# Stick-breaking attention heads taken two at a time in a two-block transformer kernel

## The chip, the cores and the metric

The kernel runs on one core of a Trainium2 chip. The metric is the device time of one execution in microseconds (us). A core has five engines, each with its own list of instructions: TensorE (PE, matmuls), VectorE (DVE), ScalarE (ACT), GpSimd (POOL) and SyncE (SP, which here only issues transfers). They meet through semaphores: an instruction can wait until a semaphore has reached a value, and can raise one when it is done. A list is worked off strictly in order, so an instruction that waits holds up everything behind it on its engine.

## The reference

Two transformer blocks run over 512 tokens of width 1024 (the second one in two layers). The change lies in the first layer of the second block, in its stick-breaking attention of 8 heads of width 64:

```python
def _stick_breaking(q, k, v):
    for blk in range(seq // QBLOCK):               # QBLOCK = 128
        t0, t1 = blk * QBLOCK, (blk + 1) * QBLOCK
        z = einsum('bhtd,bhsd->bhts', q[:, :, t0:t1], k[:, :, :t1]) * scale
        mask = arange(t1)[None, :] < arange(t0, t1)[:, None]
        log1m = where(mask, -softplus(z), 0.0)
        suffix = cumsum(log1m, axis=3, reverse=True)
        a = where(mask, exp(z + suffix), 0.0)
        outs.append(einsum('bhts,bhsd->bhtd', a, v[:, :, :t1]))
```

q and k are root-mean-square normalised per head before it. Beside this attention the same layer computes `y_a = u * mixed`, where `mixed` is a masked product of 128x128 matrices, and then multiplies both halves by an output matrix. Everything is float32.

## The kernel before

All weights stream in as chunks of 128 x 1024. SyncE loads a chunk into one of 4 buffers (`RAW`). ScalarE's `hi()` copies it, rounded, to one of 3 buffers (`WH`, L800), and VectorE's `lo()` writes what the rounding left (`WL`, L1260). A gemm then makes 3 matmuls for each of 8 slices (high x high, high x low, low x high, L279 to L281), 24 in all, on one chunk. `hi()` of chunk n waits until the gemm of chunk n - 3 is done, because it writes that chunk's buffer. Chunks have a fixed order, so each call of `hi()` and of `lo()` means the next chunk.

The 8 heads are worked in rounds `n` = 0 to 9, written out by hand in `tensor`, `scalar` and `vector`, each in a function `even()`. Work on a head goes through these steps:

- `st_a`: TensorE multiplies keys and queries (L602), 1280 score columns for a head (transposed and triangular in blocks of 128): four diagonal blocks in bank 2, the rest in banks 3 and 7. A head's key and query are 64 rows high, in rows 0 to 63 for even heads and 64 to 127 for odd ones.
- `st_z`: VectorE adds the mask to the diagonal blocks (L1560) and copies the rest (L1565) into the head's row of scores, `ZR`. ScalarE's `st_soft` computes the softplus in absolute value (L1041, L1045), exp (L1047) and log (L1049) in `SPR`; VectorE's L1568 combines. A change between exp and log, root or gelu costs ScalarE a table load.
- GpSimd adds blocks of the softplus into `TS`; TensorE's `st_b` forms the sums from the right (L615, and L622 with a matrix of ones), in banks 2, 3 and 7 again.
- `st_zd`: VectorE subtracts them from the scores (L1575); `st_exp`: ScalarE's exp (L1034).
- `st_c`: TensorE multiplies the values (L633), 64 columns wide, into the lower or upper half of bank 6. After an odd head ScalarE (`close`) and VectorE move the bank out.

Between the steps stand the gemms of the next queries and keys (`even_job`, chunks `eq` and `ek`), later of `u` (`eu`). For each pair of heads, `head_norm` (TensorE's 2-column sums L562, VectorE's L1539, ScalarE's root L809, VectorE's reciprocal) and `head_apply` (TensorE spreads the factor, L575; VectorE multiplies, L1548) normalise query and key. `st_a` waits for them through the semaphore `qkn`. A bank is reused when `open_bank` has seen the semaphore of its last reader. Before round 0, `spatial()` fills banks 4, 5, 0 and 1, which VectorE empties with four additions (L1626).

The attention of the first block (`scores`, `values`, lines L382 and L463) works on two heads at a time, in alternating halves of the array.

Of the kernel before, what the change touches and what calls it, by code (L numbers as in the profile page):

```python
# [9 lines left out]
S = 512  # L10
# [3 lines left out]
ALU = mybir.AluOpType  # L14
# [125 lines left out]
def build(nc, W, X, CV, PAR, CON, OH, LNG, LNB, SGB, SGW, RB, OUT):  # L140
    scr = nc.dram_tensor("bias_scratch", (16, 640), F32)

    with ExitStack() as ctx:
# [76 lines left out]
        QE, KE, VE, MX, VG = ar.take(4, S), ar.take(4, S), ar.take(4, S), ar.take(4, S), ar.take(4, S)  # L220
        LG, LB = CSB[:, 0:512], CSB[:, 512:1024]
        SQ2 = CSB[:, 0:512]
        SW, SBT, st, HN = ar.take(8, 128), ar.take(4, 128), ar.take(4, 16), ar.take(64)
        Z01, SP0, TS = ar.take(2, 1280), ar.take(1280), ar.take(384)
        ZR = [Z01[:, 0, :], Z01[:, 1, :], ARENA[:, 8192:8192 + 1280]]
        SPR = [SP0, ARENA[:, 8192 + 1280:8192 + 2560]]
# [44 lines left out]
        free = {}  # L271

        def tensor(e):
# [320 lines left out]
            def st_a(h):  # L594
                c, r0 = h // 2, 64 * (h % 2)
                e.wait_ge(sem["qkn"], 2 * c + 2)
                parts = [[(i, 128 * i, 128 * i + 128, 128 * i) for i in range(4)],
                         [(0, 128, 512, 0), (2, 384, 512, 384)], [(1, 256, 512, 0)]]
                for p, (part, b) in enumerate(zip(parts, (2, 3, 7))):
                    open_bank(b)  # L600
                    for i, q0, q1, c0 in part:
                        t = e.matmul(ps(b, c0, c0 + q1 - q0), KE[r0:r0 + 64, c, 128 * i:128 * i + 128],  # L602
                                     QE[r0:r0 + 64, c, q0:q1], start=True, stop=True)
                    t.then_inc(sem["sqk"])
                    free[b] = (("z", 3 * h + p + 1),)

            def st_b(h):
                L = SPR[h % 2]
# [4 lines left out]
                for p, ((lo, hi), b) in enumerate(zip(PIECES, (2, 3, 7))):  # L613
# [6 lines left out]
                for part, b in zip(later, (2, 3, 7)):  # L620
                    for m, (c0, c1, src) in enumerate(part):
                        t = e.matmul(ps(b, c0, c1), ON, src, start=False, stop=(m == len(part) - 1))  # L622
                    if part:
                        t.then_inc(sem["suf"])

            def st_c(h):
                r0 = 64 * (h % 2)
                jobs = [(i, 128 * i, 128 * i + 128, 128 * i) for i in range(4)]
                jobs += [(i, 128 * (i + 1), 512, LATE[i][0]) for i in (0, 1, 2)]
                e.wait_ge(sem["za"], h + 1)  # L630
                open_bank(6)
                for m, (i, q0, q1, z0) in enumerate(jobs):
                    t = e.matmul(PSB[6][r0:r0 + 64, q0:q1], VE[:, i, 64 * h:64 * h + 64], ZR[h % 3][:, z0:z0 + q1 - q0],  # L633
                                 start=(m == 0), stop=(m == 6))
                t.then_inc(sem["spv"])
                if h % 2:
                    free[6] = (("o_lo", 8 + h // 2 + 1),)
# [4 lines left out]
            def even():  # L642
# [12 lines left out]
                for n in range(10):  # L655
                    if 1 <= n <= 8:
                        st_b(n - 1)
                    if n < 8:
                        st_a(n)
                    if n == 0:  # L660
                        gemm([even_job(2, 0)], B)
                        gemm([even_job(3, 1)], B)
                    elif n in (1, 3, 5):
                        c = (n + 1) // 2
                        head_norm(c)
                        if c < 3:
                            gemm([even_job(2 * c + 2, 0)], B)
                        else:
                            gemm([(("eu", 0), 0, ("u_rr", 1))], B)
                        head_apply(c)  # L670
                    elif n in (2, 4):
                        gemm([even_job(n + 3, 1)], B)
                    elif n < 9:
                        gemm([(("eu", n - 5), (n - 5) % 2, ("u_rr", n - 4))], B)
                    if n >= 2:
                        if n == 2:
                            e.wait_ge(sem["tok"], 12)
                        st_c(n - 2)
# [111 lines left out]
        def scalar(e):  # L790
# [241 lines left out]
            def st_exp(h):  # L1032
                e.wait_ge(sem["zd"], 3 * h + 3)
                e.activation(ZR[h % 3], ZR[h % 3], ACT.Exp).then_inc(sem["za"])  # L1034

            def st_soft(h):
                L, Z = SPR[h % 2], ZR[h % 3]
                e.wait_ge(sem["z"], 3 * h + 1)
                if h > 1:
                    e.wait_ge(sem["suf"], 3 * (h - 2) + 3)  # L1040
                e.activation(L[:, 0:512], Z[:, 0:512], ACT.Abs).then_inc(sem["abs"])  # L1041
                for p, b in ((1, 3), (2, 7)):
                    lo, hi_ = PIECES[p]
                    e.wait_ge(sem["sqk"], 3 * h + p + 1)
                    e.activation(L[:, lo:hi_], ps(b, 0, hi_ - lo), ACT.Abs).then_inc(sem["abs"])  # L1045
                e.wait_ge(sem["abs"], 3 * h + 3)
# [11 lines left out]
            def even():  # L1058
# [30 lines left out]
                for n in range(10):  # L1089
                    if 1 <= n <= 8:  # L1090
                        st_exp(n - 1)
                    if n == 7:
                        e.wait_ge(sem["spg"], 4)
                    if n < 8:
                        st_soft(n)
                    if n == 0:
                        even_sq(2)
                        hi()
                        even_sq(3)
                    elif n in (1, 3, 5):  # L1100
                        c = (n + 1) // 2
                        head_sqrt(c)
                        hi()
                        if c < 3:
                            even_sq(2 * c + 2)
                        else:
                            eu(0)
                    elif n in (2, 4):
                        hi()
                        even_sq(n + 3)  # L1110
                    elif n < 9:
                        hi()
                        eu(n - 5)
                    if n >= 3 and n % 2:
                        m = (n - 3) // 2
                        close(A[0][:, 4 + m, :], ("spv", n - 1))
# [135 lines left out]
        def vector(e):  # L1252
# [302 lines left out]
            def st_z(h):  # L1555
                Z = ZR[h % 3]
                e.wait_ge(sem["sqk"], 3 * h + 1)
                if h > 2:
                    e.wait_ge(sem["spv"], h - 2)
                e.tensor_tensor(blocks(Z[:, 0:512], 4), blocks(ps(2), 4), bcast(cc("smask"), 4),  # L1560
                                ALU.add).then_inc(sem["z"])
                for p, b in ((1, 3), (2, 7)):
                    c0, c1 = PIECES[p]
                    e.wait_ge(sem["abs"], 3 * h + p + 1)
                    e.tensor_copy(Z[:, c0:c1], ps(b, 0, c1 - c0)).then_inc(sem["z"])  # L1565
                e.wait_ge(sem["z"], 3 * h + 3)
                e.wait_ge(sem["sln"], h + 1)
                e.scalar_tensor_tensor(SPR[h % 2], Z, 0.0, SPR[h % 2], ALU.max, ALU.add).then_inc(sem["sp"])  # L1568

            def st_zd(h):  # L1570
                Z = ZR[h % 3]
                for p, b in enumerate((2, 3, 7)):
# [12 lines left out]
            def even():  # L1585
# [42 lines left out]
                for n in range(10):  # L1628
                    if 1 <= n <= 8:
                        st_zd(n - 1)  # L1630
                    if n < 8:
                        st_z(n)
                    if n == 0:
                        even_rr(2, 0)
                        lo()
                        even_rr(3, 1)
                    elif n in (1, 3, 5):
                        c = (n + 1) // 2
                        head_norm(c)
                        lo()  # L1640
# [5 lines left out]
                    elif n in (2, 4):  # L1646
                        lo()
                        even_rr(n + 3, 1)
                    elif n < 9:
                        lo()  # L1650
                        eu(n - 5)
# [178 lines left out]
        def gpsimd(e):  # L1830
# [44 lines left out]
            for h in range(8):  # L1875
                L = SPR[h % 2]
                e.wait_ge(sem["sp"], h + 1)
                if h:
                    e.wait_ge(sem["suf"], 3 * h)
# [4 lines left out]
            e.wait_ge(sem["spv"], 8)  # L1884
# [131 lines left out]
```

## Time and profile before

| | us |
|---|---|
| median of 3 runs | 1923.31 (1922.28 to 1924.86) |
| profiled execution | 1924.35 |
| its span | 1922.5 |
| TensorE busy | 1871.0 (97%) |
| VectorE busy | 955.1 (50%) |
| ScalarE busy | 753.5 (39%) |
| GpSimd busy | 76.6 (4%) |
| mean granted TensorE clock | 0.991 |

The profile comes from one execution. "Busy" is the time in which an engine works on at least one instruction; what matters for the time is the chain of work that ended last and the waits on it. The granted clock is the share of full TensorE speed (2.4 GHz) that the chip allowed; 0.5 is 1.2 GHz. Float32 matmuls of the attention appear as two records each, so seven matmuls show as x14. The rounds changed here lie between 799 and 941 us.

### The profile page before, as it was taken

To read this page: it belongs to the slowest core of one execution; us is meant where nothing else is said; L and a number is where in the kernel's file an instruction comes from. 1 tells how busy PE (TensorE), PEld (TensorE's weight loads), DVE (VectorE), ACT (ScalarE), POOL (GpSimd) and SP (SyncE) were. 2 spreads that over 40 slices of the span, in tenths; PEclk is the share of its full clock that TensorE was granted. 3 is DMA by queue.
4 is the path that set the end of the run, shared out by engine and by line. 5 is a ranking of instruction groups with operands and counts; after the bars stand their busy time and mean duration, and the time that the engine had idled before them with its cause. 6 is when DMAs were issued, how large, how long until landed. Compare 5 with 4: busy or idle time off the path is not lost.

```text
span 1922.5 us, 21105 instructions
## 1 busy us (share of the span) xinstructions
PE 1871.0 (97%) x8624; PEld 1512.8 (79%) x8624; DVE 955.1 (50%) x1363; ACT 753.5 (39%) x1080; POOL 76.6 (4%) x94
## 2 busy tenths in 40 slices
PE   3999999899999999999999999999999999999999
PEld 2788788778888888777788888888876788888887
DVE  7377636553434455645554444345734554344343
ACT  4366542342323243466543323233446443232231
POOL 5100000000000000000000000000001000000000
PEclk9999999899999999999999999999999999999999
DMA  7455553222222223110123222222321132222322
GB/s 256 163 173 184 167 173 132 88 77 99 99 97 101 88 99 115 66 45 23 56 98 102 96 99 99 99 88 99 98 77 44 55 102 96 99 99 91 105 90 77
DMA packets 55120, 197.65 MB, mean 103 GB/s; under 512 B 6400, under 2 KB 6656, under 8 KB 55024
## 3 DMA queue, kind: packets, MB, share of 16 engines
q1 hardware_dynamic: 52272, 188.24, 28.7%
q0 software_dynamic: 2320, 7.31, 1.4%
q8 instruction: 69, 1.13, 0.2%
q10 hardware_dynamic: 432, 0.74, 0.1%
q14 instruction: 27, 0.22, 0.0%
HBM read 194.13 MB, written 2.14 MB: 102 GB/s over the span
## 4 chain that ended last, share of the span: by engine, by line
PE 93%; DVE 4%; ACT 2%; DMA 0%; issue 0%; POOL 0%; SPq 0%; ACTq 0%; DVEq 0%
PE ps L279 26%; PE ps L281 26%; PE ps L280 26%; PE ps L315 2%; PE ps L316 2%; PE ps L317 2%; DVE RAW L1268 1%; PE ps L382 1%; PE ps L615 1%; PE ps L703 1%; DVE WL L1260 1%; PE ps L602 1%; PE ps L633 1%; PE ps L333 1%; PE ps L622 1%; ACT WH L800 0%
## 5 line engine op out<-in xcount | busy, mean ns | idle before, releaser
L279 PE MATMUL ps<-R0h,WH 128*128 128x512 f32 x1200 | 472.0, 393 | 20.4 <-POOL R0l L1837 17.9
L1260 DVE TENSOR_TENSOR WL<-RAW,WH 128x1024 fp32r<-128x1024 f32 x303 | 372.4, 1233 | 215.9 <-ACT WH L800 212.2
L800 ACT ACTIVATE WH<-RAW 128x1024 fp32r<-128x1024 f32 x303 | 317.6, 1052 | 392.8 <-PE ps L281 339.5
L280 PE MATMUL ps<-R0l,WH 128*128 128x512 f32 x1200 | 468.5, 390 | 0.0
L281 PE MATMUL ps<-R0h,WL 128*128 128x512 f32 x1200 | 468.3, 390 | 0.0
L279 PE MATMUL ps<-R1h,WH 128*128 128x512 f32 x1064 | 420.5, 395 | 7.9 <-POOL R1l L1867 2.8
L280 PE MATMUL ps<-R1l,WH 128*128 128x512 f32 x1064 | 417.0, 392 | 0.0
L281 PE MATMUL ps<-R1h,WL 128*128 128x512 f32 x1064 | 416.8, 392 | 0.0
L279 PEld LDWEIGHTS ps<-R0h,WH 128*128 128x128 f32 x1200 | 226.0, 188 | 74.5 <-issue 15.2
L281 PEld LDWEIGHTS ps<-R0h,WL 128*128 128x128 f32 x1200 | 226.1, 188 | 47.5
L280 PEld LDWEIGHTS ps<-R0l,WH 128*128 128x128 f32 x1200 | 226.2, 188 | 46.1
L279 PEld LDWEIGHTS ps<-R1h,WH 128*128 128x128 f32 x1064 | 201.5, 189 | 58.2 <-issue 11.8
L281 PEld LDWEIGHTS ps<-R1h,WL 128*128 128x128 f32 x1064 | 201.5, 189 | 42.6
L280 PEld LDWEIGHTS ps<-R1l,WH 128*128 128x128 f32 x1064 | 201.7, 190 | 41.2
L1307 DVE TENSOR_TENSOR XT<-ps,XT 128x512 f32<-128x512 f32 x80 | 55.3, 691 | 192.0 <-PE ps L281 192.0
L1299 DVE TENSOR_TENSOR R0l<-TMP,R0h 128x512 fp32r<-128x512 f32 x117 | 81.0, 692 | 125.3 <-ACT R0h L997 87.4
L995 ACT ACTIVATE TMP<-TMP 128x512 f32<-128x512 f32 x64 | 40.5, 633 | 201.5 <-DVE TMP L1481 201.5
L1481 DVE SCALAR_TENSOR_TENSOR TMP<-ps,SQ 128x512 f32<-128x512 f32 x64 | 44.2, 690 | 78.0 <-PE ps L281 78.0
L1310 DVE SCALAR_TENSOR_TENSOR XT<-ps,mod,XT 128x512 f32<-128x512 f32 x40 | 29.9, 750 | 87.7 <-PE ps L281 87.7
L1268 DVE CUSTOM_DVE_ANT_0 RAW<-RAW,CSB,par 128x1024 f32<-128x1024 f32 x48 | 67.0, 1408 | 0.0
L1469 DVE TENSOR_TENSOR TMP<-TMP 128x512 f32<-128x512 f32 x32 | 22.1, 692 | 64.1 <-ACT TMP L982 64.1
L315 PE MATMUL ps<-WH,R1h 128*128 128x512 f32 x128 | 51.1, 399 | 0.0
(270 smaller groups left out, 1413.6 us busy)
## 6 DMA issues: line engine op xcount, KB each, us to landing
RAW<-in_W SPq DMA_DIRECT2D x351, 512.0 KB, 3.2
XT<-in_X SPq DMA_DIRECT2D x4, 512.0 KB, 7.8
ARENA<-bias_scratch POOLq DMA_DIRECT2D x8, 256.0 KB, 4.4
XT<-in_X POOLq DMA_DIRECT2D x8, 256.0 KB, 3.7
out_x<-XT SPq DMA_DIRECT2D x8, 256.0 KB, 2.0
ARENA<-bias_scratch POOLq DMA_DIRECT2D x8, 128.0 KB, 3.6
con<-in_CON POOLq DMA_DIRECT2D x1, 578.0 KB, 6.0
CSB<-in_CV ACTq DMA_DIRECT2D x1, 512.0 KB, 5.9
```

The source lines that it names most:

```text
L279: e.matmul(ps(b), wh, hi, start=first, stop=False)
L280: e.matmul(ps(b), wh, lo, start=False, stop=False)
L281: return e.matmul(ps(b), wl, hi, start=False, stop=last)
L315: e.matmul(ps(b), h1, wh, start=(k == 0), stop=False)
L316: e.matmul(ps(b), h1, wl, start=False, stop=False)
L800: e.activation(WH[:, n % NHL, :], RAW[:, i % NRAW, :], ACT.Copy).then_inc(sem["w_hi"])
L995: e.activation(TMP[:, j, :], TMP[:, j, :], ACT.Square).then_inc(sem["mlp_sq"])
L1260: e.tensor_tensor(WL[:, s, :], RAW[:, i % NRAW, :], r32(WH[:, s, :]), ALU.subtract).then_inc(sem["w_lo"])
L1268: e.tensor_tensor_reduce(RAW[:, r, :], RAW[:, r, :], CSB[:], 1.0, par[:, c0:c0 + 1], ALU.mult, ALU.add, mod_col(j)).then_inc(sem["ada"])
L1299: e.tensor_tensor(dst[1][:, k, :], src, r32(dst[0][:, k, :]), ALU.subtract).then_inc(sem[done])
L1307: e.tensor_tensor(XT[:, k, :], ps(b), XT[:, k, :], ALU.add).then_inc(sem[done])
L1481: e.scalar_tensor_tensor(TMP[:, j, :], ps(b), 0.0, SQ[:], ALU.max, ALU.mult).then_inc(sem["mlp_rr"])
```

## The change

Scores and values are computed for two heads at once. `st_a(m)` writes the scores of heads 2m and 2m + 1: the even head into banks 2, 3 and the left half of 7, the odd head into 4, 5 and the right half of 7, with matmuls of lower and upper rows mostly in turn, and a wait before the second write to bank 7. `st_c(c)` writes the values of both heads in turn. The sums of even heads (`st_b`) go to banks 4, 5, 6, those of odd ones to 2, 3, 7. There are now four rows of scores (`ZR`) and two sets of block sums (`TSR`). In the arena `VG`, `SW` and `SBT` share their place with one row of softplus and two rows of scores. ScalarE takes absolute values from the scores that VectorE wrote, in one instruction. The order of the steps within the rounds changes on three engines.

```diff
+        SP1, ZR2, ZR3 = (ARENA[:, at0 + 1280 * n:at0 + 1280 * n + 1280] for n in range(3))
+        Z01, SP0, TSR = ar.take(2, 1280), ar.take(1280), ar.take(2, 384)
+        ZR = [Z01[:, 0, :], Z01[:, 1, :], ZR2, ZR3]
...
-            def st_a(h):
+            def st_a(m):
+                def part(e_, i, q0, q1, b, c0):
+                    r = slice(64 * e_, 64 * e_ + 64)
+                    return e.matmul(ps(b, c0, c0 + q1 - q0), KE[r, m, 128 * i:128 * i + 128], QE[r, m, q0:q1],
+                                    start=True, stop=True)
+                def diag(e_, i):
+                    return part(e_, i, 128 * i, 128 * i + 128, 2 + 2 * e_, 128 * i)
+                e.wait_ge(sem["qkn"], 2 * m + 2)
+                for b in (7, 4):
                     open_bank(b)
+                part(0, 1, 256, 512, 7, 0).then_inc(sem["sqk"])
+                diag(1, 0)
+                diag(1, 1)
+                for b in (3, 5):
+                    open_bank(b)
+                part(0, 0, 128, 512, 3, 0)
+                part(1, 0, 128, 512, 5, 0)
+                part(0, 2, 384, 512, 3, 384).then_inc(sem["sqk"])
+                part(1, 2, 384, 512, 5, 384).then_inc(sem["sqk"])
+                open_bank(2)
+                diag(0, 0)
+                e.wait_ge(sem["sqk"], 6 * m + 1)
+                part(1, 1, 256, 512, 7, 256).then_inc(sem["sqk"])
+                diag(0, 1)
+                for i in (2, 3):
+                    t0 = diag(0, i)
+                    t1 = diag(1, i)
...
             def st_b(h):
+                banks = (2, 3, 7) if h % 2 else (4, 5, 6)
...
-            def st_c(h):
+            def st_c(c):
-                e.wait_ge(sem["za"], h + 1)
+                e.wait_ge(sem["za"], 2 * c + 2)
                 open_bank(6)
                 for m, (i, q0, q1, z0) in enumerate(jobs):
+                    for h in (2 * c, 2 * c + 1):
+                        r0 = 64 * (h % 2)
+                        t = e.matmul(PSB[6][r0:r0 + 64, q0:q1], VE[:, i, 64 * h:64 * h + 64],
+                                     ZR[h % 4][:, z0:z0 + q1 - q0], start=(m == 0), stop=(m == 6))
...
                 for n in range(10):                      # TensorE
-                    if 1 <= n <= 8:
-                        st_b(n - 1)
-                    if n < 8:
-                        st_a(n)
+                    if n % 2:
+                        if n < 9:
+                            st_b(n - 1)
+                    elif n < 8:
+                        st_a(n // 2)
+                    else:
+                        st_b(7)
...
-                    if n >= 2:
+                    if n in (2, 4, 6):
+                        st_b(n - 1)
+                    if n % 2 and n >= 3:
...
-                        st_c(n - 2)
+                        st_c((n - 3) // 2)
...
                 for n in range(10):                      # ScalarE
-                    if 1 <= n <= 8:
-                        st_exp(n - 1)
-                    if n < 8:
-                        st_soft(n)
+                    if n == 8:
+                        hi()
+                        st_exp(7)
+                    elif n % 2 == 0:
+                        hi()
+                        st_soft(n)
+                    elif n < 9:
+                        if n > 1:
+                            st_exp(n - 2)
+                        if n < 6:
+                            head_sqrt((n + 1) // 2)
+                        hi()
+                        st_exp(n - 1)
+                        st_soft(n)
...
                 for n in range(10):                      # VectorE
-                    if 1 <= n <= 8:
+                    if n == 8:
+                        st_zd(7)
+                    elif n % 2 == 0:
+                        st_z(n)
+                        st_z(n + 1)
+                    elif n < 9:
+                        if n > 1:
+                            st_zd(n - 2)
                         st_zd(n - 1)
+                        if n < 6:
+                            head_norm((n + 1) // 2)
+                    if n < 9:
+                        lo()
                     if n < 8:
-                        st_z(n)
+                        st_sp(n)
```

`st_sp` is the combination of the softplus, before the last lines of `st_z`. After it VectorE goes on with `even_rr` or `eu` and `head_apply` as before.

How the order moves on ScalarE at round 0, before:

```order
L800 ACTIVATE WH<-RAW 128x1024 [waits mm,raw2]
L1041 ACTIVATE ARENA<-ARENA 128x512 [waits z]
L1045 ACTIVATE ARENA<-ps3 128x512 [waits sqk]
L1045 ACTIVATE ARENA<-ps7 128x256 [waits sqk]
L1047 ACT_TABLE_LOAD
L1047 ACTIVATE ARENA<-ARENA 128x1280 [waits abs]
L1049 ACT_TABLE_LOAD
L1049 ACTIVATE ARENA<-ARENA 128x1280 [waits sxp]
```

And after, at the same place (L832 is the weight copy, L1073 the absolute value, L1075 the exp, L1077 the log, L1062 the squares for the head sums, L841 the root):

```order
L832 ACTIVATE WH<-RAW 128x1024 [waits mm,raw2]
L832 ACTIVATE WH<-RAW 128x1024 [waits mm,raw3]
L1073 ACTIVATE ARENA<-ARENA 128x1280 [waits z]
L1075 ACT_TABLE_LOAD
L1075 ACTIVATE ARENA<-ARENA 128x1280 [waits abs]
L1077 ACT_TABLE_LOAD
L1077 ACTIVATE ARENA<-ARENA 128x1280 [waits sxp]
L1062 ACTIVATE TMP<-ARENA 128x512 [waits hss,eqk] x2
```

The weight copy from `raw3` stood behind the softplus, between the two squares; now it stands ahead of the softplus. It waits (`mm`) for the first gemm of round 0.

VectorE from the sums of head 0 to the next pair's halves, before (L1575 subtracts the sums, L1568 combines the softplus of head 1, L1539 and L1543 are `head_norm`, L1533 is `even_rr`, L1548 `head_apply`):

```order
L1575 TENSOR_TENSOR ARENA<-ARENA,ps7 128x256 [waits suf]
L1560 TENSOR_TENSOR ARENA<-ps2,con 128x512 [waits sqk]
L1565 COPY ARENA<-ps3 128x512 [waits abs]
L1565 COPY ARENA<-ps7 128x256 [waits abs]
L1568 SCALAR_TENSOR_TENSOR ARENA<-ARENA 128x1280 [waits sln,z]
L1539 TENSOR_SCALAR ARENA<-ps2 128x8 [waits hss] x2
L1543 RECIPROCAL ARENA<-ARENA 128x16 [waits hsqrt]
L1260 TENSOR_TENSOR WL<-RAW,WH 128x1024 [waits w_hi]
L1533 TENSOR_TENSOR ARENA<-ps0,SQ 128x512 [waits mm]
L1548 SCALAR_TENSOR_TENSOR ARENA<-ARENA,par,ps3 128x512 [waits hspr]
L1548 SCALAR_TENSOR_TENSOR ARENA<-ARENA,par,ps7 128x512 [waits hspr]
```

And after, in the same order of steps (L1600, L1564, L1568, L1285, L1593, L1558, L1573):

```order
L1600 TENSOR_TENSOR ARENA<-ARENA,ps6 128x256 [waits suf]
L1564 TENSOR_SCALAR ARENA<-ps2 128x8 [waits hss] x2
L1568 RECIPROCAL ARENA<-ARENA 128x16 [waits hsqrt]
L1285 TENSOR_TENSOR WL<-RAW,WH 128x1024 [waits w_hi]
L1593 SCALAR_TENSOR_TENSOR ARENA<-ARENA 128x1280 [waits z,sln]
L1558 TENSOR_TENSOR ARENA<-ps0,SQ 128x512 [waits mm]
L1573 SCALAR_TENSOR_TENSOR ARENA<-ARENA,par,ps3 128x512 [waits hspr]
L1573 SCALAR_TENSOR_TENSOR ARENA<-ARENA,par,ps7 128x512 [waits hspr]
L1585 TENSOR_TENSOR ARENA<-ps2,con 128x512 [waits sqk]
```

The combination stood ahead of the two `head_norm` instructions; now it stands between them and `head_apply`.

TensorE's first scores, before (five rows for head 0):

```order
L602 MATMUL ps2<-ARENA 128x128 [waits hn,qkn]
L602 MATMUL ps2<-ARENA 128x128 x3
L602 MATMUL ps3<-ARENA 128x384 [waits qkn]
L602 MATMUL ps3<-ARENA 128x128
L602 MATMUL ps7<-ARENA 128x256 [waits qkn]
```

And after, for heads 0 and 1:

```order
L602 MATMUL ps7<-ARENA 128x256 [waits mx,qkn]
L602 MATMUL ps4<-ARENA 128x128 x2
L602 MATMUL ps3<-ARENA 128x384 [waits mx,qkn]
L602 MATMUL ps5<-ARENA 128x384
L602 MATMUL ps3<-ARENA 128x128
L602 MATMUL ps5<-ARENA 128x128
L602 MATMUL ps2<-ARENA 128x128 [waits hn]
L602 MATMUL ps7<-ARENA 128x256 [waits sqk]
```

The first scores now wait for `mx`, which VectorE's additions of L1626 raise (L1651 after).

## Rows read from the trace of the kernel before

**Rows 1.** The page: busy time by engine, and the chain that ended last by engine.

```profile
PE 1871.0 (97%) x8624; PEld 1512.8 (79%) x8624; DVE 955.1 (50%) x1363; ACT 753.5 (39%) x1080; POOL 76.6 (4%) x94
PE 93%; DVE 4%; ACT 2%; DMA 0%; issue 0%; POOL 0%; SPq 0%; ACTq 0%; DVEq 0%
```

**Rows 2.** The view by windows, the changed rounds: length, busy by engine, clock, DMA.

```profile
core 0: us, PE busy (x) PEld busy (x) DVE busy (x) ACT busy (x) POOL busy (x), PEclk, DMA share, GB/s
799.00:946.00 147.00, 144.41 (x760) 109.96 (x757) 75.28 (x112) 93.14 (x103) 14.10 (x26) 0.95 0.11 38
```

**Rows 3.** TensorE's waits from 799 to 946 us: total, times, longest.

```profile
PE ps L279 <- DVE ARENA L1626: 2.1, 1, 2.1
PE ps L615 <- DVE ARENA L1548: 0.5, 1, 0.5
```

**Rows 4.** TensorE's timeline, round 1 and part of 2: start, us, engine, line.

```profile
821.13 2.46 PE L602 MATMUL ps<-ARENA 64*128 64x128 f32 x14
823.52 1.95 PE L562 MATMUL ps<-con,TMP 128*128 128x2 f32 x16
825.33 0.48 PE L279 MATMUL ps<-R1h,WH 128*128 128x512 f32 x1
...
830.99 1.97 PE L575 MATMUL ps<-con,ARENA 128*64 128x128 f32 x32
...
844.73 2.38 PE L633 MATMUL ps<-ARENA 128*64 128x128 f32 x14
```

**Rows 5.** TensorE's timeline, first block: values, then scores, two heads each.

```profile
194.95 2.37 PE L463 MATMUL ps<-ARENA 128*64 128x512 f32 x16
197.25 2.95 PE L382 MATMUL ps<-ARENA 64*128 64x512 f32 x16
```

**Rows 6.** VectorE's timeline, rounds 0 and 1.

```profile
801.63 2.48 DVE L1626 TENSOR_TENSOR ARENA<-ps,ARENA 128x512 f32<-128x512 f32 x4
...
811.40 1.49 DVE L1568 SCALAR_TENSOR_TENSOR ARENA<-ARENA 128x1280 f32<-128x1280 f32 x1 [4.50 <-ACT ARENA L1049]
812.81 0.68 DVE L1533 TENSOR_TENSOR ARENA<-ps,SQ 128x512 f32<-128x512 f32 x1
...
829.85 0.23 DVE L1539 TENSOR_SCALAR ARENA<-ps 128x8 f32<-128x8 f32 x2
...
833.06 1.40 DVE L1548 SCALAR_TENSOR_TENSOR ARENA<-ARENA,par,ps 128x512 f32<-128x512 f32 x2
```

**Rows 7.** ScalarE's timeline: softplus, weight copy, root, and a gelu of `eu`.

```profile
806.14 1.28 ACT L1047 ACT_TABLE_LOAD   x1
807.44 1.27 ACT L1047 ACTIVATE ARENA<-ARENA 128x1280 f32<-128x1280 f32 x1
808.73 1.28 ACT L1049 ACT_TABLE_LOAD   x1
810.02 1.27 ACT L1049 ACTIVATE ARENA<-ARENA 128x1280 f32<-128x1280 f32 x1
...
814.07 1.04 ACT L800 ACTIVATE WH<-RAW 128x1024 fp32r<-128x1024 f32 x1
...
823.05 0.63 ACT L1041 ACTIVATE ARENA<-ARENA 128x512 f32<-128x512 f32 x1
823.59 0.85 ACT L1045 ACTIVATE ARENA<-ps 128x512 f32<-128x512 f32 x2
...
830.12 0.22 ACT L809 ACTIVATE ARENA<-ARENA 128x16 f32<-128x16 f32 x1 [0.49 <-DVE ARENA L1539]
...
897.58 0.63 ACT L1054 ACTIVATE TMP<-TMP 128x512 f32<-128x512 f32 x1 [0.59 <-DVE TMP L1580]
```

**Rows 8.** TensorE around its two slow stretches, then windows with the granted clock.

```profile
803.65 0.77 PE L279 MATMUL ps<-R1h,WH 128*128 128x512 f32 x1 [2.13 <-DVE ARENA L1626]
...
850.71 2.46 PE L602 MATMUL ps<-ARENA 64*128 64x128 f32 x14
853.10 2.60 PE L562 MATMUL ps<-con,TMP 128*128 128x2 f32 x16
...
804.00:810.00 6.00, 6.00 (x15) 4.69 (x15) 1.72 (x4) 5.22 (x6) 0.00 (x0) 0.51 0.01 3
853.00:861.00 8.00, 8.00 (x30) 6.75 (x30) 3.03 (x7) 7.29 (x9) 1.29 (x3) 0.57 0.00 1
```

More of the change, by code:

```diff
@@ L592, in spatial @@
                     free[b] = (("mx", gp + 1),)
-            def st_a(h):
[L595 to L599, printed above, removed]
-                    open_bank(b)
[L601 to L605, printed above, removed]
+            def st_a(m):
[7 more added lines that the diff above has]
+                for b in (7, 4):
+                    open_bank(b)
+                part(0, 1, 256, 512, 7, 0).then_inc(sem["sqk"])
[15 more added lines that the diff above has]
+                    t1 = diag(1, i)
+                t0.then_inc(sem["sqk"])
+                t1.then_inc(sem["sqk"])
+                for b, z in ((2, 1), (3, 2), (7, 6), (4, 4), (5, 5)):
+                    free[b] = (("z", 6 * m + z),)
@@ L612, in st_b @@
                 e.wait_ge(sem["sp"], h + 1)
-                for p, ((lo, hi), b) in enumerate(zip(PIECES, (2, 3, 7))):
+                for p, ((lo, hi), b) in enumerate(zip(PIECES, banks)):
                     open_bank(b)
@@ L619, in st_b @@
                 e.wait_ge(sem["ts"], 3 * h + 3)
-                for part, b in zip(later, (2, 3, 7)):
+                for part, b in zip(later, banks):
                     for m, (c0, c1, src) in enumerate(part):
@@ L1097, in even @@
                         even_sq(2)
-                        hi()
                         even_sq(3)
[L1100 to L1109, printed above, removed]
+                    elif n < 5:
                         even_sq(n + 3)
                     elif n < 9:
-                        hi()
                         eu(n - 5)
@@ L1555, in st_z, with st_sp @@
             def st_z(h):
[L1556 to L1560, printed above, removed]
+                Z, up = ZR[h % 4], h % 2
+                if h > 3:
+                    e.wait_ge(sem["spv"], h // 2 - 1)
+                e.wait_ge(sem["sqk"], 6 * (h // 2) + 5 + up)
+                e.tensor_tensor(blocks(Z[:, 0:512], 4), blocks(ps(2 + 2 * up), 4), bcast(cc("smask"), 4),
                                 ALU.add).then_inc(sem["z"])
[L1562 to L1565, printed above, removed]
+                e.tensor_copy(Z[:, 512:1024], ps(3 + 2 * up)).then_inc(sem["z"])
+                e.tensor_copy(Z[:, 1024:1280], ps(7, 256 * up, 256 * up + 256)).then_inc(sem["z"])
+            def st_sp(h):
+                e.wait_ge(sem["sln"], h + 1)
                 e.wait_ge(sem["z"], 3 * h + 3)
-                e.wait_ge(sem["sln"], h + 1)
-                e.scalar_tensor_tensor(SPR[h % 2], Z, 0.0, SPR[h % 2], ALU.max, ALU.add).then_inc(sem["sp"])
+                e.scalar_tensor_tensor(SPR[h % 2], ZR[h % 4], 0.0, SPR[h % 2], ALU.max, ALU.add).then_inc(sem["sp"])
             def st_zd(h):
-                Z = ZR[h % 3]
-                for p, b in enumerate((2, 3, 7)):
+                Z = ZR[h % 4]
+                for p, b in enumerate((2, 3, 7) if h % 2 else (4, 5, 6)):
                     c0, c1 = PIECES[p]
@@ L1875, in gpsimd @@
             for h in range(8):
-                L = SPR[h % 2]
+                L, TS = SPR[h % 2], TSR[:, h % 2, :]
                 e.wait_ge(sem["sp"], h + 1)
-                if h:
-                    e.wait_ge(sem["suf"], 3 * h)
+                if h > 1:
+                    e.wait_ge(sem["suf"], 3 * h - 3)
                 e.tensor_tensor(TS[:, 256:384], L[:, 896:1024], L[:, 384:512], ALU.add).then_inc(sem["ts"])
```

46 lines of the change are left out of this document (16 added, 30 removed).

## The prediction

> **What bounds the kernel now.** I read the page first: TensorE is busy 97% of the span and holds 93% of the chain that ended last [rows 1]. A microsecond off or on TensorE in any stage is therefore a microsecond of the time, unless something else already holds the engine there. The change touches one stage, the stick-breaking heads, so I read next the windows from 799 to 946 us: TensorE 144.4 of 147 us, ScalarE 93, VectorE 75 [rows 2]. The waits of that stretch say what else there is: TensorE waited for data only twice, 2.1 us for an addition on VectorE and 0.5 us for the scaled heads [rows 3]. So the other two engines have slack on average; whether they still have it in the new order is the whole question. Third comes TensorE's timeline of one round, for prices [rows 4]. Last the granted clock: two stretches of this stage run at half speed (1.2 instead of 2.4 GHz), one after the 2.13 us wait, one after a score group of 64 rows followed by the sixteen 2-column matmuls of the head sums [rows 8].
>
> **Part 1: paired scores and values.** Before, a head's scores use 64 rows of the array and take 2.46 us; a head's values use 64 columns and take 2.38 us [rows 4]. There are 8 of each: 19.7 and 19.0 us. The first block already works in pairs: its values of two heads, alternating between the output halves, as many columns in all as two of these groups, took 2.37 us together, and its scores of two heads 2.95 us [rows 5]. One group of one head costs what two of them do when they alternate. The new scores alternate a little better than those of the first block but are cut into 14 matmuls instead of 8, with one wait of TensorE for its own first matmul, so I take 2.6 us a pair, and 2.5 us for a pair of values (bounds for each 2.37 and 2.95). Saved: 19.7 - 4 x 2.6 = 9.3 and 19.0 - 4 x 2.5 = 9.0, together 18.3 us (bounds 15.1 and 19.8). If pairs did not overlap here it would be nothing.
>
> **Part 2: the start.** TensorE reaches the first scores at 799.06 (803.65 - 2.13 - 2.46, [rows 8, 4]). Before, it does them first and then waits 2.13 us for bank 0. Now they also write bank 4, which is free only once the first addition of L1626 is done, 801.63 + 0.62 = 802.25 [rows 6]. The wait is 3.2 us: +1.1.
>
> **Part 3: round 0 to 1.** ScalarE's list now has the weight copy `hi()` ahead of the softplus of head 0, where before it was behind it. That copy waits until the first of the two gemms that follow is done (three weight buffers). Before, the softplus ran beside that gemm. Now, from its end: copy 1.04, absolute value 1.3 (before in pieces of 0.63 and 0.85), table load 1.28, exp 1.27, table load 1.28, log 1.27 [rows 7], VectorE's combination 1.49 [rows 6], 0.2 for the hops: 9.1 us. TensorE has one gemm of 5.5 us beside it (825.33 to 830.99 less its start, [rows 4]) and then stands at the sums of head 0: 3.6 us.
>
> **Part 4: odd rounds into even ones.** `st_a(1)` needs both normalised halves of the next pair, written by `head_apply`. Before, VectorE did the combination of its head, then `head_norm`, weight rest, `even_rr`, `head_apply`: no softplus lay between the head sums and the apply. Now the combination stands between `head_norm` and `head_apply`, and it waits for a softplus that ScalarE starts only after root, weight copy and the exp of the head before. From the end of the head sums: VectorE 0.23, root 0.22, copy 1.04, load 1.28, exp 1.27, absolute value 1.3, exp 1.27, load 1.28, log 1.27, combination 1.49, scaling 0.68, apply 1.40 [rows 6, 7], hops 0.3: 13.0. Beside it TensorE has gemm 5.5 and spread 1.9 [rows 4]: it waits 5.5 us before the second pair's scores. Before the third pair a value pair (2.5) lies in between as well: 3.0 us. Before the fourth pair the apply stands behind `eu(0)`, four more steps of 0.6 to 0.7 (one is in [rows 7]): 3.0 + 2.6 = 5.6 us.
> Round 7 to 8: from the end of the sums of head 6, VectorE's subtraction waits behind `eu(1)`, then exp, copy, exp, softplus (5.1) and combination follow; 11.4 us against gemm and value pair, 7.9: 3.5 us. In rounds 3, 5 and 7 the second head of a pair finishes about 0.5 us late: 1.5 in all.
>
> **Sum at full clock.** Waits added: 1.1 + 3.6 + 5.5 + 3.0 + 5.6 + 3.5 + 1.5 = 23.8 us; removed the 0.5 us of [rows 3], since scores now ask for the normalised halves at another place. 23.8 - 0.5 - 18.3 = +5.0 us. The extra tiles (a fourth row of scores, a second set of partial sums) take waits away on VectorE and GpSimd that were on nobody's path: 0. The whole-tile absolute value replaces three, from SBUF: within 0.2 us, counted above. TensorE's matmul count and every DMA stay.
>
> **The clock.** From 804 to 810 us the granted clock averages 0.51, from 853 to 861 it averages 0.57 [rows 8]; the first is all inside a slow stretch, the second holds 0.43 x 2 x 8 = 6.9 us of one. At half speed such a stretch costs half its length, 3.4 us, if TensorE is busy throughout. The trace shows a fall after a wait of 2.13 us and none after 0.5 us [rows 3, 8]. The new order has six waits of 3 us and more where there was one of 2.1. I count one fall for each, and take 2.6 us rather than 3.4, since part of a slow stretch lies in the wait itself or beside a ScalarE chain that then ends earlier relative to TensorE: 15.6 us. The two falls of before (6.8 us) lie in its own time; the second one stood behind half-row scores next to the head sums, a neighbourhood that is gone. Net +8.8 us; bounds 0 (as many falls as before) and 13.6 (six at 3.4).
> The Trainium skill (TensorE: Matmul & The Clock Gate, "Why this matters for your kernels") says to leave no idle gaps between matmul bursts, or the clock goes back to half. By that rule the savings of pairing are not there to be had while these gaps open; the trace agrees, by the fall after 2.13 us. The sum above does not rest on it.
>
> **Result.** 5.0 + 8.8 = +13.8 us on the profiled execution, 1924.35 us (span 1922.5 and 1.85 around it): 1938.2. The three timed runs have their median 1.0 lower, at 1923.31, so the forecast is 1937.
>
> A page and the trace differ on one price in the chains. The Trainium skill (ScalarE: Activation LUTs, "What ACT_TABLE_LOAD costs") puts a switch of table sets at about 2.66 us, 1.28 for the load and the rest for a drain. Here the load takes 1.28 us and the exp begins at its end (806.14 + 1.28, [rows 7]), so the measurement decides. By the page's figure each of the five chains, with two loads, would be 2.8 us longer, 14 us in all.
>
> **The rivals.**
> (a) *Falls of the clock stay at two or fewer.* Waits as above, clock as before: 1924.35 + 5.0 = 1929. For it: waits of 3 us are spread among full-array gemms, and paired matmuls fill the array. Against: the fall after 2.13 us. 15%.
> (b) *Faster: the chains are covered.* The mechanism is ScalarE's list in round 0 and VectorE's in round 1: if the weight copy did not wait for the gemm and the apply's chain took under 7.4 us, what TensorE has beside it, the waits would shrink to the start's +1.1 and the savings stand: 1924.35 - 18.3 + 1.1 = 1907. For it: ScalarE is busy 63% and VectorE 51% of the stage [rows 2]. Against: the chain is 13.0 us by single rows, and would have to lose 5.6. A partial form, chains some 3 us shorter in five places, would end near no change. Faster 4%, near no change 4%.
> (c) *The pairs do not overlap*, so the change does not do what it says on TensorE: 18.3 us are not saved, and the chains are no shorter: 1955. Against: [rows 5]. 3%.
> (d) *The table switches cost what the page says.* Two on each chain, 2.8 us longer in five places: 1951. Against: exp starts as the load ends in [rows 7]. 2%.
> The forecast itself, five or six falls, has 72%.
>
> **How the numbers follow.** The measurement of this kernel can tell about 0.2%, 3.8 us, from no change. Slower: forecast 72, (a) 15, (c) 3, (d) 2: 92%. Same 4%, faster 4%, both from (b). The likeliest case by its own bounds (savings 15.1 to 19.8 us, clock +5 to +13.6) runs from 1924.35 + 23.3 - 19.8 + 5 = 1933 to 1924.35 + 23.3 - 15.1 + 13.6 = 1946. The range takes in (a): 1928 to 1946.
>
> **What would show it.** In the profile after: the score group of a pair at 2.4 to 2.9 us with twice the matmuls, the value group at 2.4 to 2.6. TensorE's waits in the stage near 24 us instead of 2.6 of [rows 3], on VectorE's combination (round 1, round 8) and on its apply (rounds 2, 4, 6). Softplus of head 0 beginning about 1 us after the end of the first gemm. More stretches at half clock between 800 and 960. VectorE and ScalarE busy as before. Wrong would be: no wait over 1 us at the second pair's scores (b); a pair at 4.5 us or more (c); waits as said but the clock down only twice (a).

## The result, and the profile after

| | before | after |
|---|---|---|
| median of 7 runs, us | 1923.31 (1922.28 to 1924.86) | 1930.33 (1929.22 to 1934.18) |
| profiled execution, us | 1924.35 | 1930.21 |
| its span | 1922.5 | 1928.3 |

The ratio is 1.0041, 95% interval 1.0029 to 1.0052: slower by 0.4%. TensorE is busy less than before and waits more. From the profile page of the kernel after, to be set beside [rows 1]:

```profile
PE 1852.9 (96%) x8624; PEld 1502.4 (78%) x8624; DVE 953.4 (49%) x1363; ACT 754.6 (39%) x1066; POOL 72.9 (4%) x94
PE 89%; DVE 5%; ACT 4%; issue 1%; DMA 1%; POOL 0%; SPq 0%; ACTq 0%; DVEq 0%
```

TensorE is busy 18 us less in the whole and holds 89% of the chain that ended last instead of 93%. The waits of TensorE in the changed rounds, 795 to 955 us (total, times, longest; compare [rows 3]):

```profile
PE ps L602 <- DVE ARENA L1573: 14.0, 3, 5.8
PE ps L642 <- DVE ARENA L1593: 8.0, 4, 3.6
PE ps L602 <- DVE ARENA L1651: 3.3, 1, 3.3
```

That makes 25.3 us instead of 2.6: three waits of the scores (L602) for `head_apply` (L1573), four of the sums (L642) for the combination of the softplus (L1593), one for the first addition. TensorE's timeline shows where each stands, and what the paired groups take:

```profile
801.79 4.10 PE L602 MATMUL ps<-ARENA 64*128 64x256 f32 x28 [3.32 <-DVE ARENA L1651]
820.62 2.42 PE L642 MATMUL ps<-ARENA,con 128*128 128x512 f32 x6 [3.63 <-DVE ARENA L1593]
838.70 4.41 PE L602 MATMUL ps<-ARENA 64*128 64x256 f32 x28 [5.18 <-DVE ARENA L1573]
852.80 2.42 PE L642 MATMUL ps<-ARENA,con 128*128 128x512 f32 x6 [0.55 <-DVE ARENA L1593]
865.56 2.34 PE L661 MATMUL ps<-ARENA 128*64 128x128 f32 x28
870.88 4.64 PE L602 MATMUL ps<-ARENA 64*128 64x256 f32 x28 [2.99 <-DVE ARENA L1573]
906.11 4.64 PE L602 MATMUL ps<-ARENA 64*128 64x256 f32 x28 [5.79 <-DVE ARENA L1573]
920.51 2.42 PE L642 MATMUL ps<-ARENA,con 128*128 128x512 f32 x6 [0.48 <-DVE ARENA L1593]
935.40 3.84 PE L642 MATMUL ps<-ARENA,con 128*128 128x512 f32 x6 [3.35 <-DVE ARENA L1593]
948.29 0.50 PE L283 MATMUL ps<-R0h,WH 128*128 128x512 f32 x1
```

A value pair takes 2.34 to 2.39 us, as one head did in [rows 4]. A score pair takes 4.10 to 4.64 us: right behind its wait it runs at half clock. Windows, with the granted clock behind the POOL column; the last one holds the 3.63 us wait and the sums behind it, and there the clock stayed full:

```profile
802.00:805.00 3.00, 3.00 (x19) 2.46 (x21) 1.44 (x3) 0.00 (x0) 0.00 (x0) 0.50 0.03 5
835.00:843.00 8.00, 4.30 (x28) 3.71 (x28) 3.41 (x4) 1.73 (x3) 1.28 (x3) 0.57 0.00 0
870.00:877.00 7.00, 6.12 (x32) 5.10 (x33) 2.79 (x6) 1.56 (x3) 0.22 (x1) 0.51 0.02 4
904.00:911.00 7.00, 4.89 (x29) 4.15 (x30) 2.79 (x5) 1.40 (x2) 0.00 (x0) 0.51 0.00 0
816.60:827.00 10.40, 6.77 (x39) 5.14 (x38) 4.89 (x9) 5.59 (x7) 1.28 (x3) 1.00 0.01 4
```

ScalarE's timeline of round 0 shows the weight copy (L832) that now stands ahead, with the wait that held up the softplus behind it, and then the steps of the softplus end to end:

```profile
811.65 1.06 ACT L832 ACTIVATE WH<-RAW 128x1024 fp32r<-128x1024 f32 x1 [15.15 <-PE ps L285]
812.61 1.26 ACT L1073 ACTIVATE ARENA<-ARENA 128x1280 f32<-128x1280 f32 x1
813.89 1.28 ACT L1075 ACT_TABLE_LOAD   x1
815.19 1.28 ACT L1075 ACTIVATE ARENA<-ARENA 128x1280 f32<-128x1280 f32 x1
816.48 1.28 ACT L1077 ACT_TABLE_LOAD   x1
817.77 1.27 ACT L1077 ACTIVATE ARENA<-ARENA 128x1280 f32<-128x1280 f32 x1
```

The rounds, from the end of `spatial()` to the first output gemm, take 801.79 - 3.32 = 798.47 to 948.29, 149.8 us; before, from 799.06 to the row below, 142.2. They cost 7.6 us more. The rest of the span is 1.8 us shorter, in stretches that the change does not touch.

```profile
941.30 0.50 PE L279 MATMUL ps<-R0h,WH 128*128 128x512 f32 x1
```

### The profile page after: what moved, and what is told of

It is laid out like the page before. It is cut to its first block, busy times and chain, and to the rows that moved or that the text cites. A ratio compares the mean times of both kernels' runs of the same rounds, so it can differ in the third digit from the quotient of the medians.

```text
span 1928.3 us, 21089 instructions
## 1 busy us (share of the span) xinstructions
PE 1852.9 (96%) x8624; PEld 1502.4 (78%) x8624; DVE 953.4 (49%) x1363; ACT 754.6 (39%) x1066; POOL 72.9 (4%) x94
## 4 chain that ended last, share of the span: by engine, by line
PE 89%; DVE 5%; ACT 4%; issue 1%; DMA 1%; POOL 0%; SPq 0%; ACTq 0%; DVEq 0%
PE ps L283 26%; PE ps L284 25%; PE ps L285 25%; PE ps L319 2%; PE ps L320 2%; PE ps L321 2%; DVE RAW L1293 1%; PE ps L386 1%; PE ps L602 1%; PE ps L735 1%; PE ps L642 1%; ACT WH L832 1%; DVE WL L1285 1%; DVE ARENA L1593 1%; PE ps L337 1%
## 5 line engine op out<-in xcount | busy, mean ns | idle before, releaser
L1285 DVE TENSOR_TENSOR WL<-RAW,WH 128x1024 fp32r<-128x1024 f32 x303 | 372.2, 1232 | 215.4 <-ACT WH L832 211.5
L832 ACT ACTIVATE WH<-RAW 128x1024 fp32r<-128x1024 f32 x303 | 317.7, 1052 | 408.6 <-PE ps L285 354.7
```

The source lines that it names most:

```text
L832: e.activation(WH[:, n % NHL, :], RAW[:, i % NRAW, :], ACT.Copy).then_inc(sem["w_hi"])
L1285: e.tensor_tensor(WL[:, s, :], RAW[:, i % NRAW, :], r32(WH[:, s, :]), ALU.subtract).then_inc(sem["w_lo"])
```

## The experiments

The theory: pairing saves what it should on TensorE (T1), the time is lost in waits that come from the order of the steps on VectorE and ScalarE (T2), and in half-clock stretches that these waits bring (T3). The rivals: pairs do not save; the waits only move when one is removed; the half clock is independent of them. Each ratio below is to the kernel before, timed beside the run on the same chip: 1924.4 us beside the apply-first, copy-later, additions-first and fill runs, 1923.8 beside fill-all and exp-later, 1924.1 beside the others. The changed kernel's 1930.3 us stand beside 1923.3 (ratio 1.0041). So a difference to the changed kernel is uncertain by about 1 us more than the spread of the medians; where that matters the ratios decide.

### Is it the order? (T2)

**Apply first.** VectorE's `head_apply` ahead of the combination in rounds 1, 3 and 5, and in round 5 ahead of `eu(0)` as well:

```diff
-                    if n < 8:
+                    if n < 8 and n not in (1, 3, 5):
                         st_sp(n)
...
                             even_rr(2 * c + 2, 0)
-                        else:
+                        head_apply(c)
+                        st_sp(n)
+                        if c == 3:
                             eu(0)
-                        head_apply(c)
```

> The changed kernel, with VectorE's head_apply ahead of the softplus combination st_sp in rounds 1, 3 and 5. Theory (the lost time is waits made by the new order): the waits before the second, third and fourth pair's scores (5.2, 3.0, 5.8 us) shrink to about 1, 0 and 0 us, some 2 us come back before the sums in round 7, and the slow stretches behind them go, so the scores of pairs 1 to 3 take 2.6 us instead of 4.4 to 4.6: 1930.3 - 12 - 6 = 1912 us, 1908 to 1918. Rival (TensorE's own work grew: pairs do not save what they should, and waits only move elsewhere): within 3 us of 1930.

Measured 1913.87 us (ratio to before 0.995, 0.9937 to 0.9962), 16.5 less than the changed kernel. In its timeline the waits before the scores are 0.90, 0 and 0 us, and the scores of the later pairs run at full clock:

```profile
835.42 2.46 PE L602 MATMUL ps<-ARENA 64*128 64x256 f32 x28 [0.90 <-DVE ARENA L1573]
862.55 2.46 PE L602 MATMUL ps<-ARENA 64*128 64x256 f32 x28
889.78 2.46 PE L602 MATMUL ps<-ARENA 64*128 64x256 f32 x28
904.41 3.87 PE L642 MATMUL ps<-ARENA,con 128*128 128x512 f32 x6 [3.02 <-DVE ARENA L1593]
```

The last row is what came back: 3.0 us ahead of the sums in round 7, where 2 were expected, with a slow stretch behind them. One place in VectorE's list thus decides between slower and faster than before. TensorE's own work is not the cause.

**Copy later.** ScalarE in round 0 (VectorE's `lo()` likewise moves behind the combination and the step after it):

```diff
+                    elif n == 0:
+                        st_soft(n)
+                        hi()
```

> The changed kernel, with the softplus of head 0 ahead of the weight copy in round 0 on ScalarE, and its combination ahead of the rest of that chunk on VectorE. Theory: the 3.6 us wait before the sums of head 0 goes to under 1 us, no clock fall was tied to it: 1930.3 - 3.0 = 1927.3 us, 1925.5 to 1928.5. Rival (the later chain through the ScalarE copies takes it back at the next wait): 1930.

Measured 1927.88 us (ratio 1.002, 1.0011 to 1.0029; the changed kernel had 1.0029 to 1.0052). The 3.63 us wait before the sums of head 0 is gone; the later waits stay at 5.15, 3.02 and 5.79 us:

```profile
817.64 2.31 PE L642 MATMUL ps<-ARENA,con 128*128 128x512 f32 x6
835.60 4.64 PE L602 MATMUL ps<-ARENA 64*128 64x256 f32 x28 [5.15 <-DVE ARENA L1576]
```

What was won there was kept: 2.4 us by the medians, 3.5 against the kernel before beside each.

**Additions first.** VectorE ahead of round 0: the loop over L1651 before the last five `scale_x`.

> The changed kernel, with VectorE's four additions that empty banks 4, 5, 0, 1 ahead of its last five scalings. Theory: the 3.3 us wait before the first scores goes, and the slow stretch with it (1.7 us): 1930.3 - 5 = 1925.3 us, 1924 to 1927.5. Rival (the scalings, now later, delay the first pair's masks and the time returns in the wait before the sums of head 0, since ScalarE only starts after the first gemm anyway): no more than 1 us gained.

Measured 1926.81 us (ratio 1.0015, 1.0006 to 1.0024), 3.5 less. The first score pair follows without a wait and runs at full clock, but the slow stretch now begins later, at the sums of head 0, behind their wait:

```profile
799.18 2.61 PE L602 MATMUL ps<-ARENA 64*128 64x256 f32 x28
816.53 3.79 PE L642 MATMUL ps<-ARENA,con 128*128 128x512 f32 x6 [3.63 <-DVE ARENA L1593]
```

So 3.3 us of wait went and little of the half clock: the time fell into the expected range, but the slow stretch did not go, as the theory had it.

### Is it the pairing? (T1)

**Scores in blocks.** Same banks, but all matmuls of the even head ahead of those of the odd one:

```diff
+                part(0, 0, 128, 512, 3, 0)
+                part(0, 2, 384, 512, 3, 384).then_inc(sem["sqk"])
+                for i in range(4):
+                    t0 = diag(0, i)
+                for b in (4, 5):
                     open_bank(b)
-                part(0, 0, 128, 512, 3, 0)
                 part(1, 0, 128, 512, 5, 0)
...
-                for i in (2, 3):
-                    t0 = diag(0, i)
+                for i in range(4):
                     t1 = diag(1, i)
```

> The changed kernel, with the scores of a pair not in turn: all matmuls of the even head, then all of the odd one, same banks. Theory (alternating halves overlap): a pair at full clock costs 4.7 us instead of 2.6, at half clock up to 9, so 4 x 2.1 at least and 4 x 4 at most: 1930.3 + 8 to 16 = 1942 us. Rival (the array overlaps halves however they are ordered, or not at all): within 2 us of 1930.

Measured 1941.94 us (ratio 1.0095, 1.0082 to 1.0109), 11.6 more. A pair in a half-clock stretch takes 8.19 us instead of 4.64:

```profile
843.42 8.19 PE L602 MATMUL ps<-ARENA 64*128 64x256 f32 x28 [5.15 <-DVE ARENA L1569]
```

The 11.6 us are not the price of the order alone. This profile holds 44 us at half clock in the rounds where that of the kernel after holds 27, and 19.8 us of waits instead of 25.3.

**Values in blocks.** The seven matmuls of one head ahead of the other's:

```diff
-                for m, (i, q0, q1, z0) in enumerate(jobs):
-                    for h in (2 * c, 2 * c + 1):
+                for h in (2 * c, 2 * c + 1):
+                    for m, (i, q0, q1, z0) in enumerate(jobs):
```

> The changed kernel, with the values of a pair not in turn: the seven matmuls of the even head, then those of the odd one. Theory: a value pair costs 3.9 to 4.6 us instead of 2.34. Rounds 3, 5 and 7 have a wait of 3.0 to 5.8 us right behind it (scores of the next pair, sums of head 7) that is set by VectorE's and ScalarE's chains, so three of the four are hidden in those waits and only the last one costs: 1930.3 + 2 = 1932 us, 1930 to 1934. Rival (all four on the path): 1930.3 + 8 = 1938 us.

Measured 1931.58 us, 1.3 more than the changed kernel, at the same ratio of 1.0041 (1.0029 to 1.0054): no difference that can be told. A pair takes 3.91 us instead of 2.34, and the wait behind it shrinks by the same 1.5 us, from 2.99 to 1.46:

```profile
866.43 3.91 PE L661 MATMUL ps<-ARENA 128*64 128x128 f32 x28
871.80 2.46 PE L602 MATMUL ps<-ARENA 64*128 64x256 f32 x28 [1.46 <-DVE ARENA L1573]
```

Alternating saves on both groups. In the changed kernel three of the four savings on the values are only waited for again: the waits behind them were 2.99, 5.79 and 3.35 us and are 1.46, 4.22 and 1.77 here. The fourth, in round 9, should then cost 1.6 us, but the total does not isolate it: this profile also holds only 14 us at half clock in the rounds, against 27, and 2.4 us more outside them.

### Is the half clock tied to the waits? (T3)

**Fill.** Matmuls that nobody reads, into bank 7 or 1, ahead of the even rounds:

```diff
+                    if n % 2 == 0:
+                        fill(1 if n else 7, {0: 13, 2: 21, 4: 12, 6: 23, 8: 13}[n])
```

> The changed kernel, with matmuls on data that nobody reads put into TensorE's waits before rounds 0, 2, 4, 6 and 8 (13, 21, 12, 23, 13 of 128x512, 0.23 us each), so that it stands still only shortly. All waits for data remain. Theory (the slow stretches are tied to the waits and fall on the scores): scores of a pair at 2.5 to 2.7 us in all four, the granted clock 1.00 from 799 to 950 us, 1930.3 - 9 = 1921 us, 1919 to 1924. Rival (the slow stretches do not depend on the waits, or half-array work alone causes them): 1930 or more, with the same slow stretches.

Measured 1925.58 us (ratio 1.0006, 0.9997 to 1.0014), 4.7 less and not the 9 expected, outside the stated range. The four score pairs take 2.46 to 2.62 us as forecast, with every wait for data still in place. But a slow stretch, from 819.6 to 826.5, came with the one long wait that was left open, 3.63 us in round 1:

```profile
820.23 4.63 PE L642 MATMUL ps<-ARENA,con 128*128 128x512 f32 x6 [3.63 <-DVE ARENA L1600]
...
841.35 2.46 PE L602 MATMUL ps<-ARENA 64*128 64x256 f32 x28 [0.17 <-DVE ARENA L1580]
```

**Fill all.** The same, with `fill(7, 15)` ahead of round 1.

> The kernel of e4_fill with the one long wait that it left open, before the sums of head 0 in round 1 (3.63 us), filled as well (15 more matmuls that nobody reads). In e4_fill's profile the only slow stretch of these rounds stood right behind that wait. Theory (each long wait can bring a fall, and only they do): no slow stretch between 799 and 950 us, 1925.6 - 3.4 = 1922 us, 1920.5 to 1923.5. Rival (a slow stretch comes anyway, at the next half-array or 2-column work, as it did when the first wait was taken out of the kernel before): 1925.6.

Measured 1922.55 us (ratio 0.9994, 0.9986 to 1.0003), 7.8 less than the changed kernel. The granted clock of the rounds is 1.00 in its profile; that of the kernel after was 0.91 (one window of 151 us each, the filled kernel first):

```profile
799.00:950.00 151.00, 148.09 (x884) 116.14 (x880) 73.67 (x112) 94.41 (x89) 10.46 (x26) 1.00 0.12 39
```

```profile
799.00:950.00 151.00, 126.24 (x743) 98.67 (x744) 71.60 (x110) 94.13 (x89) 10.38 (x26) 0.91 0.10 35
```

The kernel still waits for the same chains, and only the clock differs; in its profile the rounds take 140.7 us instead of 149.8 (799.19 to 939.88). The whole price of the half clock is 7.8 us, as large as the 7.0 us that the changed kernel lost. But the kernel before pays for half clock too, so the slowdown is not all clock; the sum is in the next section.

**The kernel before, additions first.** The same move as in the third run, made in the kernel before.

> The kernel before, with VectorE's four additions ahead of its last five scalings. Theory: the 2.1 us wait and the slow stretch behind it (3.4 us) go: 1923.3 - 5.5 = 1917.8 us, 1916 to 1920. Rival (the slow stretch only moves to the next half-array work): 1923.3 - 2.1 = 1921 us.

Measured 1922.90 us, ratio 0.9994 (0.9985 to 1.0003): no change that can be told. This expectation failed, and its rival, that the slow stretch only moves, held for the stretch. The 2.13 us wait is gone, but 1.0 and 0.3 us come back in round 1, and the slow stretch moved instead of going. Its window, and TensorE's timeline ahead of it:

```profile
819.00:826.00 7.00, 7.00 (x25) 5.87 (x24) 2.29 (x3) 6.84 (x8) 0.00 (x0) 0.51 0.01 2
```

```profile
816.96 2.62 PE L602 MATMUL ps<-ARENA 64*128 64x128 f32 x14 [1.02 <-DVE ARENA L1575]
819.51 3.57 PE L562 MATMUL ps<-con,TMP 128*128 128x2 f32 x16
```

The neighbourhood is that of the second fall in [rows 8]: scores of 64 rows, then 2-column sums, here with a 1 us wait ahead, there with none. So a fall does not need a long wait. That these groups bring it is not shown: the same two groups ran at full clock at 821.13 us in [rows 4].

### A version that beats both

**All three reorderings.**

> The changed kernel with the three reorderings of the first three runs together (head_apply ahead of the combination, softplus of head 0 ahead of the weight copy, additions ahead of the scalings). Theory: of 25 us of waits 6 to 10 remain, mainly in rounds 7 and 8, with at most one slow stretch; the savings of pairing (19 us) stand: 1930.3 - 21 = 1909 us, 1905 to 1913, below the kernel before by 14. Rival (what is won at one place is waited for at the next, since ScalarE's chain is the limit): 1920 or more.

Measured 1906.80 us (ratio to before 0.9912, 0.9898 to 0.9925). Of the 25.3 us of TensorE's waits in the rounds 7.9 are left (total, times, longest), and one slow stretch of 3.4 us, behind the wait of 3.0 us in round 7.

```profile
PE ps L642 <- DVE ARENA L1596: 6.7, 5, 3.0
PE ps L602 <- DVE ARENA L1576: 0.9, 1, 0.9
PE ps L283 <- DVE WL L1288: 0.3, 1, 0.3
```

**And the exp later.** ScalarE in odd rounds:

```diff
                         hi()
-                        st_exp(n - 1)
                         st_soft(n)
...
+                    if n % 2 and n < 9:
+                        st_exp(n - 1)
```

> The kernel of e8_all with, in rounds 1, 3, 5 and 7, ScalarE's exp of the even head (needed only for the values two rounds later) behind the softplus of the odd head and the squares or gelu after it, instead of ahead of the softplus. Theory (what remains of the waits in rounds 2, 3, 5, 7 and 8 is ScalarE's chain to the next combination, now 1.27 us shorter, and the table load for it): waits from 7.9 to about 6, the slow stretch behind the last one gone or shorter: 1906.8 - 3 = 1904 us, 1901 to 1906. Rival (the exp put later delays the squares and gelu, and the time comes back through head_apply or the values): 1907 or more.

Measured 1904.01 us (ratio 0.9898, 0.9883 to 0.9913), the fastest: 26 us below the changed kernel and 20 below the one before. The waits for the combination fell from 6.7 us to 4.8, in rounds 1, 7 and 8:

```profile
PE ps L642 <- DVE ARENA L1597: 4.8, 3, 3.2
```

The slow stretch at the wait of round 7 stayed, from 894.1 to 897.5 us, though it was expected to shrink or go.

## Why the prediction was right, and where it was off

The direction, the cause and the range held: slower by 7.0 us, where +13.8 was forecast with a range from 1928 to 1946. But 1930.3 lies below the 1933 to 1946 that the forecast's likeliest case gave by its own bounds; it is inside the range because that was widened for rival (a), whose mechanism did not occur. The clock's share was forecast more than twice too large. By its steps:

| step | forecast, us | profile after |
|---|---|---|
| score pair at full clock | 2.6 | 2.46 to 2.62 (with the waits filled or gone) |
| value pair | 2.5 | 2.34 to 2.39 |
| saved by pairing, all | 18.3 | 19.2 (what closes the sum) |
| wait at the first scores | 3.2 | 3.32 |
| before the sums of head 0 | 3.6 | 3.63 |
| before pairs 2, 3, 4 | 5.5, 3.0, 5.6 | 5.18, 2.99, 5.79 |
| before the sums of head 7 | 3.5 | 3.35 |
| late second heads | 1.5 | 0.55 + 0.48 |
| clock, net | +8.8 | +4.1 |

**The waits** came within 0.5 us each, and the savings within 0.9 in all. A chain of work read row by row from the kernel before, set against what TensorE has beside it in the new order, gave each wait although the trace of before shows none of them. The chain of Part 4, 13.0 us in the forecast, took 12.7: from the end of the head sums (826.04) to the scores at 838.70. The run with `head_apply` first shows that the order on VectorE caused the three waits ahead of pairs 2, 3 and 4; ahead of pair 4 it moved `eu(0)` too, and the two shares were not separated. Two slips in the working did no harm. The "near 24 us" of waits to be seen is what the sum adds, while its own terms make 25.9 with the 2.1 us that the start had before. And of the 11.4 us from round 7 to 8 only 10.2 come from rows; the rest, for the subtraction and its place, has none.

**The clock** is the term that was mis-sized. The prediction put it at six falls of 2.6 us, less the 6.8 of before. The profile has five in these rounds: the wait of 3.63 us brought none there (it did in the fill and the additions-first run). Two of the five lasted 3.4 us, not 6.8, and part of the others lay in the waits themselves. By fine windows TensorE was busy under half clock for 3.4, 4.0, 6.0, 4.9 and 3.0 us, 21.3 in all, costing half, 10.7. By the same measure the two stretches of before hold 6.2 and 6.9 us busy and cost 6.6, so the clock's net is +4.1. Waits 25.3 - 2.6, savings 19.2 and clock 4.1 make the 7.6 us that the rounds cost more. The savings are here what closes the sum; by the rows the value pairs saved 19.0 - 9.5 = 9.5 us and the score pairs, at the full-clock 2.46 to 2.62, another 9.2 to 9.9, so all of it is seen. The full-clock part is thus +3.5, where the forecast had +5.0. The 1.8 us gained outside the rounds belong to no step: the records of the granted clock hold some 20 us at half clock there before and 14 after, in code that is the same.

**Rival (a)**, clock falls at two or fewer, lies nearest in time, 1929 against 1930.3, but by luck: it had the net of the clock at nothing and two falls at most. There were five, and filling all waits, which removed them, took off 7.8 us. **Rival (b)**, the chains are covered, did not hold for the order as it was. The reordered kernels are close to it, with 1906.8 and 1904.0 where it gave 1907, though the nearness is partly chance: with all three moves 7.9 us of waits are left and not 3.2, and most of the half clock that it took as staying is gone. **Rival (c)** fell in the profile, with pairs of 2.34 and, at full clock, 2.46 us, and with the scores in blocks. **Rival (d)** fell in the profile: behind the weight copy the absolute value, load, exp, load and log follow end to end (813.89 + 1.28 = 815.17, exp at 815.19), and the wait came at 3.63 us, not 3.6 + 2.8. On the Trainium skill's rule about idle gaps (TensorE: Matmul & The Clock Gate, "Why this matters for your kernels"): the runs agree in part. With the long waits filled the falls were gone. But the fall that the prediction took for agreement came behind 2.13 us, a shorter gap than the rule names, the kernel before falls at 854 us with no wait ahead [rows 8], with its first wait removed it falls at 819 behind one of 1 us, and a wait of 3.63 us brought none in the kernel after.

Left open: why a wait of 3.63 us brings a fall in some of these kernels and none in others, what brings the falls without one, what the extra tiles are worth by themselves, and how much of the last 20 us is the pairing, since no run put single heads into lists as well ordered.

## What to carry to other kernels

When work is made faster by batching two units, each engine's list must be reordered for the new distance between producer and consumer: write down, per hand-over, the chain on the other engines and what the bound engine has beside it, and move first whatever stands in the chain without being needed by it. Here the place of one call in VectorE's list was worth 16.5 us, over twice the whole slowdown. A wait on TensorE can have a second price, since it can bring half clock just when the awaited work starts; to see which part of a loss that is, fill the wait with matmuls that nobody reads and keep all the waits for data.

## What the runs showed of the hardware

- Float32 matmuls on opposite row halves, in turn, overlap nearly in full: 2.46 us for two heads in 14 matmuls, as much as one head alone in 7 [rows 4]. Grouped by head most of the overlap is gone: 8.19 against 4.64 us at half clock.
- On opposite column halves, grouped by head, two value groups took 3.91 us, less than twice 2.38 and more than the 2.34 in turn: some overlap is there without alternating.
- TensorE fell to half clock at 854 us in the kernel before with no wait ahead, and at 819 us in its variant behind a wait of 1.02 us, both times around the change from 64-row scores to 2-column sums; the same groups kept full clock elsewhere. In that variant, removing one wait moved a slow stretch by 16 us (from 803.0 to 819.1) and saved nothing that could be measured.
